# Second wo block in quarters back to back, both transposes and logits behind it, norms interleaved differently

## The chip, the cores and the metric

The kernel runs on one core of one Trainium2 chip. The metric is the device time of a launch in microseconds. Three runs of the kernel before took 1452.72 to 1453.64 us, 1453.02 us in the median.

## The reference

One layer of a hybrid encoder block on 256 tokens of width 1024, in f32. A first part (input projection, chunked attention, a state-space branch, cross-attention) ends in `merged`. The second part is a mixture of experts. The stretch between them is what this case is about:

```python
x = x + merged @ w_out[l]
# moe_ffn(rms_norm(x, norm_ffn[l]), ...):
logits = (xt @ w_router + b_router).astype(jnp.float32)
top_val, top_idx = lax.top_k(logits, TOP_K)          # 4 of 32
wts = jax.nn.softmax(top_val, axis=-1)
# tokens are sorted into blocks by expert; for each block:
g = jnp.minimum(xblk @ w_gate[e] + b_gate[e], SWIGLU_LIMIT)
u = jnp.clip(xblk @ w_up[e] + b_up[e], -SWIGLU_LIMIT, SWIGLU_LIMIT)
yb = ((u + 1.0) * g * jax.nn.sigmoid(SWIGLU_ALPHA * g)) @ w_down[e] + b_down[e]
```

## The kernel before

The tokens lie in two tiles of 128 (t = 0, 1). The first part is a list of weight blocks of 512 columns, each in four quarters of 256 input rows. A quarter ("unit") is loaded, rounded by ScalarE (`split`), its rest is taken by VectorE or GpSimd (`rest`), and TensorE runs three passes with the two parts (`three_passes`, L1589 to L1593). A list written out by `schedule()` (L93 to L208) orders everything: each engine walks it and does its own share of each step. `at(w, ...)` puts a step behind unit w. The last two blocks are `("wo", 0)` and `("wo", 1)`, the two column halves of w_out.

Block wo1 is special. The steps of the list run its four quarters for token tile 0 only; the four quarters of tile 1 (`second_tile(q)`) are written behind the list. Between them lie the transposes of x (step `outT` for columns 0 to 511 of both tiles, `turn_out(t)` for the rest of tile t) and the router's products (step `logits` for the first four chunks of both tiles, `last_logits(t)` for the last four). TensorE's order from wo1 on (L1868 to L1902) is: q0, q1, q2, `outT`, q3, `logits`, second 0, `turn_out(0)`, second 1, `last_logits(0)`, second 2, second 3, `open_sum(0, 0)`, `turn_out(1)`, count places of tile 0, `open_sum(1, 0)`, `last_logits(1)`, a small product, first gather, `open_sum(0, 1)`, two small products, second gather, `open_sum(1, 1)`, expert 0. (`open_sum` puts x into the bank that collects the result; `gather` collects the rows of expert 0 by a product with zeros and ones.)

VectorE (L1464 to L1483) does `add_out(t)` (x plus the product, for wo1's columns), `take_xT(t)` (copies transposes out of PSUM), `norm_begin(t)` (mean square), `choose(t)` (inverse root, scaled logits, top 8, row of zeros and ones), `find_first(t)` (hits of expert 0). ScalarE (L875 to L885) squares and sums a row's second half, takes the root, and scales the normed rows `h2`, tile by tile.

The expert weights come by SyncE's queue. An expert needs six loads of 2 MB in this order: gate, up, down, two halves of each. There are ten slots, and load k of expert e takes slot (6e+k) mod 10. In what follows (e,k) is load k of expert e, counted from 0. The queue (L569 to L600) waits before each load until its slot is free: load (1,0) for two quarters of wo1's tile 1 (`unit_used` at UNITS-2), (1,1) and (1,2) for all of it, (1,3) for the last logits, for `h2` and for the fourth `open_sum`, and from (1,4) on for the expert before to have used the slot. (2,2), for instance, takes slot 4, which the first down half of expert 0 holds.

Of the kernel before, what the change touches and what calls it, by code (L numbers as in the profile page):

```python
# [5 lines left out]
P = 128  # L6
# [5 lines left out]
ALU = mybir.AluOpType  # L12
# [80 lines left out]
def schedule():  # L93
# [104 lines left out]
    at(first("wo", 1) + 2, "outT")  # L198
    at(first("wo", 1) + 3, "logits")
# [45 lines left out]
def hybrid_block_kernel(nc, x, mem, g_mix, w_in, w_dt, a_gains, rel_rev, conv_w, conv_b, dt_bias, a_log, d_skip,  # L245
                        g_ssm, g_mem, w_mem_kv, x_gains, w_br_a, w_br_b, w_br_c, w_out, norm_ffn, w_router,
                        b_router, w_gate, b_gate, w_up, b_up, w_down, b_down, bias_dram, out):
    with ExitStack() as ctx:
# [420 lines left out]
        def _(act):  # L669
# [28 lines left out]
            for step in SCHED:  # L698
# [28 lines left out]
                elif kind == "take" and step[1] == "wo":  # L727
                    i = step[2]
                    cols = slice(i * NB, (i + 1) * NB)
                    for h in range(2):  # L730
                        act.wait_ge(gemm_taken, GEMM_AT[("wo", i, h)] + 1)
                        act.wait_ge(sem("br_merged"), 12)
                        act.activation(tmp[:, h], x_sb[:, h, cols], ACT.Square, accum_out=ss_part[:, 2 * i + h:2 * i + h + 1])\
                            .then_inc(sem("out_squares"), 1)
                elif kind == "take" and step[1:] != ("bc", 1):
# [139 lines left out]
            for t in range(TT):  # L875
                act.wait_ge(gemm_taken, GEMM_AT[("wo", 1, t)] + 1)
                act.wait_ge(sem("out_squares"), TT + t)
                act.activation(tmp[:, t], x_sb[:, t, NB:2 * NB], ACT.Square, accum_out=ss_part[:, TT + t:TT + t + 1])\
                    .then_inc(sem("out_squares"), 1)
                root(1)  # L880
                act.wait_ge(sem("second_norm"), t + 1)
                for h in range(2):
                    cols = slice(h * NB, (h + 1) * NB)
                    act.activation(h2[:, t, cols].rearrange("q (c p) -> q c p", c=4), interleaved(x_sb[:, t, cols]),
                                   ACT.Copy, scale=rs_2[:, t:t + 1]).then_inc(sem("h2_ready"), 1)  # L885
# [29 lines left out]
        def _(dve):  # L915
# [39 lines left out]
            def rstd_here(dst, src, width):  # L955
# [12 lines left out]
                return last  # L968

# [17 lines left out]
            for step in SCHED:  # L987
# [366 lines left out]
                elif kind == "take" and step[1] == "wo":  # L1354
# [4 lines left out]
                    for h in range(2):  # L1359
                        n = GEMM_AT[("wo", i, h)]  # L1360
                        dve.tensor_tensor(x_sb[:, h, cols], x_sb[:, h, cols], ps[:, GEMM_BANKS[n % 4], :], ALU.add)\
                            .then_inc(gemm_taken, 1)
                    dve.wait_ge(gain2_landed, 32)
                    dve.tensor_tensor(wr_sb[:], wr_sb[:], gain2_sb[:].unsqueeze(2).to_broadcast([P, KC, EXPERTS]),
                                      ALU.mult).then_inc(sem("router_scaled"), 1)
                elif kind == "outT":
                    for c2 in range(2):
# [29 lines left out]
            across = [P, TOP_K, EXPERTS]  # L1397

            def add_out(t):

                n = GEMM_AT[("wo", 1, t)]
                if t == 0:
                    dve.wait_ge(sem("wo_first_tile"), 1)
                else:
                    dve.wait_ge(unit_used, UNITS)
                dve.tensor_tensor(x_sb[:, t, NB:2 * NB], x_sb[:, t, NB:2 * NB], ps[:, GEMM_BANKS[n % 4], :], ALU.add)\
                    .then_inc(gemm_taken, 1)

            def take_xT(t):

                b = group()
                dve.tensor_copy(xT[:, 4:8, t * P:(t + 1) * P], ps[:, b, :].rearrange("p (c t) -> p c t", c=4))\
                    .then_inc(misc_taken, 1)

            def norm_begin(t):

                dve.wait_ge(sem("out_squares"), TT + t + 1)
                link(dve.tensor_tensor(ss_2[:, t:t + 1], ss_part[:, t:t + 1], ss_part[:, TT + t:TT + t + 1], ALU.add))
                variance(rs_2[:, t:t + 1], ss_2[:, t:t + 1], D)

            def choose(t):

                inverse_root(rs_2[:, t:t + 1]).then_inc(sem("second_norm"), 1)
                dve.wait_ge(sem("second_norm"), t + 1)
# [39 lines left out]
            add_out(0)  # L1464
            take_xT(0)
            norm_begin(0)
            choose(0)
            add_out(1)
            take_xT(1)
            norm_begin(1)  # L1470
            find_first(0)
# [89 lines left out]
        def _(pe):  # L1561
# [39 lines left out]

            pe.wait_ge(sem("masks"), 3)
            n = 0
            for step in SCHED:
# [8 lines left out]
                elif kind == "gemm":  # L1613
# [39 lines left out]
                    if closes:  # L1653
                        n += 2
                elif kind == "headT":
# [157 lines left out]
                elif kind == "outT":  # L1813
                    pe.wait_ge(gemm_taken, GEMM_AT[("wo", 0, 1)] + 1)
                    for c2 in range(2):
                        by_columns(lambda t: x_sb[:, t], c2)
                elif kind == "logits":
# [11 lines left out]

            def second_tile(q):  # L1830

                w = first("wo", 1) + q
                hi, lo = quarter(w)[1:]
                b = GEMM_BANKS[GEMM_AT[("wo", 1, 1)] % 4]
                for c in range(2):
                    k = 2 * q + c
                    last = three_passes(ps[:, b, :], (mergedT[0][:, k, P:T], mergedT[1][:, k, P:T]),
                                        (hi[:, c], lo[:, c]), k == 0, k == KC - 1)
                last.then_inc(unit_used, 1)

            def turn_out(t):

                b = group()
                pe.wait_ge(gemm_taken, GEMM_AT[("wo", 1, t)] + 1)
                for c in range(4):
                    last = turn(ps[:, b, c * P:(c + 1) * P], x_sb[:, t, (4 + c) * P:(5 + c) * P])
                last.then_inc(misc_ready, 1)
# [20 lines left out]
            second_tile(0)  # L1868
            turn_out(0)
            second_tile(1)  # L1870
            last_logits(0)
            second_tile(2)
            second_tile(3)
            pe.wait_ge(gemm_taken, GEMM_AT[("wo", 1, 0)] + 1)
            open_sum(0, 0)
            turn_out(1)
# [4 lines left out]
            pe.wait_ge(gemm_taken, GEMM_END)  # L1881
            open_sum(1, 0)
            last_logits(1)
# [176 lines left out]
```

## Time and profile before

| what | value |
|---|---|
| median of three runs | 1453.02 us |
| the profiled execution, its own time | 1452.76 us |
| its span | 1450.6 us |
| TensorE busy | 1426.2 us (98%) |
| VectorE / ScalarE / GpSimd busy | 587.3 / 405.6 / 63.2 us |
| moved by DMA | 491.27 MB, mean 339 GB/s |
| expert 0 starts on TensorE | 536.84 us |

The span is the time between the first and the last recorded instruction; the device time of the same execution is 2.2 us longer. Times inside the trace are from the start of the span. TensorE is recorded as busy while a matmul is in its pipeline, so a high share doesn't say that it runs at its peak. The DMA row counts how much of the core's 16 DMA engines was busy.

### The profile page before, as it was taken

The numbers are of one execution on the slowest core, as the hardware profiler recorded it, in microseconds if no ns is written. First come the engines' busy times: TensorE is split into PE (matmuls) and PEld (weight loads), VectorE is DVE, ScalarE is ACT, GpSimd is POOL, SyncE is SP. The second block draws the span as 40 slices with busy tenths as digits, with TensorE's granted clock in tenths as the row PEclk, the third lists the DMA queues.
The fourth block names the chain that finished last, engine by engine and source line by source line (L and its number), as shares of the span: only waits on it lengthen the run. The fifth ranks groups of instructions, "written<-read, shape, count | busy, mean of one in ns | idle before, by whom it ended". The sixth has DMA issues, their size and how long they took to land.

```text
span 1450.6 us, 18622 instructions
## 1 busy us (share of the span) xinstructions
PE 1426.2 (98%) x7575; PEld 820.9 (57%) x7575; DVE 587.3 (40%) x1149; ACT 405.6 (28%) x601; POOL 63.2 (4%) x50
## 2 busy tenths in 40 slices
PE   6999999999999999999999999999999999999998
PEld 6898888877788864444444444444444444433433
DVE  5779788677788651211111121121212111111111
ACT  5766666556644531101010110101011011101100
POOL 5120000111100000000000000000000000000000
PEclk9999999999999999999999999999999999999999
DMA  7455444654573979999999999999999999999997
GB/s 253 141 187 176 158 144 151 209 164 160 174 269 130 381 282 422 430 427 427 427 430 428 427 427 430 429 427 428 429 429 428 428 429 428 427 428 429 429 426 295
DMA packets 74000, 491.27 MB, mean 339 GB/s; under 512 B 5264, under 2 KB 8976, under 8 KB 49376
## 3 DMA queue, kind: packets, MB, share of 16 engines
q1 hardware_dynamic: 71280, 487.57, 83.1%
q10 hardware_dynamic: 2160, 2.62, 0.6%
q8 instruction: 32, 0.52, 0.1%
q0 software_dynamic: 512, 0.43, 0.1%
q14 instruction: 16, 0.13, 0.0%
HBM read 488.93 MB, written 1.07 MB: 338 GB/s over the span
## 4 chain that ended last, share of the span: by engine, by line
PE 82%; DMA 9%; DVE 5%; ACT 2%; issue 1%; DVEq 0%; ACTq 0%; SPq 0%
PE ps L1930 26%; PE ps L1968 13%; PE ps L1591 8%; PE ps L1593 8%; PE ps L1592 8%; PE ps L1858 7%; DMA regions<-in_w_gate 6%; PE ps L1578 4%; PE ps L1910 4%; DMA regions<-in_w_up 3%; DVE regions L1166 2%; DVE splits L1020 1%; PE ps L1805 1%; PE ps L1938 1%; ACT splits L707 1%
## 5 line engine op out<-in xcount | busy, mean ns | idle before, releaser
L1930 PE MATMUL ps<-regions,sig 128*64 128x512 f32 x2048 | 463.3, 594 | 4.1 <-DMA regions<-in_w_gate 3.8
L1930 PEld LDWEIGHTS ps<-regions,sig 128*64 128x64 f32 x2048 | 141.7, 137 | 276.7 <-issue 260.1
L1968 PE MATMUL ps<-regions,tmp 128*64 128x512 f32 x1024 | 225.1, 592 | 0.0
L1591 PE MATMUL ps<-splits,regions_r 128*128 128x512 f32 x512 | 205.9, 402 | 0.1
L1593 PE MATMUL ps<-splits,regions_r 128*128 128x512 f32 x512 | 200.1, 391 | 0.0
L1592 PE MATMUL ps<-splits,regions_r 128*128 128x512 f32 x512 | 199.8, 390 | 0.0
L707 ACT ACTIVATE splits<-halves 128x1024 fp32r<-128x1024 f32 x152 | 159.1, 1056 | 95.9 <-PE ps L1593 81.0
L1020 DVE TENSOR_TENSOR splits<-halves,splits 128x1024 fp32r<-128x1024 f32 x132 | 161.1, 1224 | 43.5 <-ACT splits L707 42.2
L893 ACT ACTIVATE work<-work 128x512 f32<-128x512 f32 x32 | 20.1, 629 | 474.9 <-DVE work L1518 474.9
L1968 PEld LDWEIGHTS ps<-regions,tmp 128*64 128x64 f32 x1024 | 71.7, 137 | 132.0 <-issue 129.6
L1858 PEld LDWEIGHTS ps<-craw,regions 128*128 128x128 f32 x1024 | 119.2, 192 | 25.6 <-issue 25.2
L1858 PE MATMUL ps<-craw,regions 128*128 128x64 f32 x1024 | 124.7, 275 | 0.4 <-DVE craw L1445 0.4
L1523 DVE TENSOR_SCALAR work<-ps 128x512 f32<-128x512 f32 x32 | 22.1, 692 | 239.7 <-PE ps L1930 239.7
L1591 PEld LDWEIGHTS ps<-splits,regions_r 128*128 128x128 f32 x512 | 96.2, 188 | 22.5 <-issue 3.9
L1593 PEld LDWEIGHTS ps<-splits,regions_r 128*128 128x128 f32 x512 | 96.1, 188 | 20.9
L1532 DVE COPY sig<-ps 128x512 f32<-128x512 f32 x32 | 22.1, 692 | 211.1 <-PE ps L1968 211.1
L1592 PEld LDWEIGHTS ps<-splits,regions_r 128*128 128x128 f32 x512 | 96.3, 188 | 18.4
L898 ACT ACTIVATE tmp<-ps 128x512 f32<-128x512 f32 x32 | 19.1, 597 | 303.1 <-PE ps L1578 303.1
L1518 DVE TENSOR_SCALAR work<-ps 128x512 f32<-128x512 f32 x32 | 22.1, 692 | 176.8 <-PE ps L1930 176.8
L1910 PE MATMUL ps<-sig,craw 64*128 64x512 f32 x264 | 65.6, 615 | 0.8 <-DVE sig L1532 0.8
L662 POOL TENSOR_TENSOR splits<-halves,splits 128x1024 fp32r<-128x1024 f32 x20 | 48.5, 2425 | 330.7 <-ACT splits L707 330.7
L1591 PE MATMUL ps<-regions_r,splits 128*128 128x256 f32 x192 | 55.5, 289 | 0.0
(299 smaller groups left out, 1188.4 us busy)
## 6 DMA issues: line engine op xcount, KB each, us to landing
regions<-in_w_gate SPq DMA_DIRECT2D x64, 2048.0 KB, 29.1
regions<-in_w_up SPq DMA_DIRECT2D x64, 2048.0 KB, 27.4
regions<-in_w_down SPq DMA_DIRECT2D x64, 2048.0 KB, 30.2
halves<-in_w_in SPq DMA_DIRECT2D x48, 1024.0 KB, 5.1
halves<-in_w_br_b SPq DMA_DIRECT2D x8, 1024.0 KB, 5.0
halves<-in_w_mem_kv SPq DMA_DIRECT2D x8, 1024.0 KB, 5.0
halves<-in_w_br_a SPq DMA_DIRECT2D x4, 1024.0 KB, 5.2
halves<-in_w_br_c SPq DMA_DIRECT2D x4, 1024.0 KB, 7.5
```

What stands on the lines that cost most here:

```text
L662: pool.tensor_tensor(lo, raw, hi.bitcast(F32), ALU.subtract).then_inc(lo_ready_pool, 1)
L707: act.activation(hi, raw, ACT.Copy).then_inc(hi_ready, 1)
L1020: dve.tensor_tensor(lo, raw, hi.bitcast(F32), ALU.subtract).then_inc(lo_ready, 1)
L1166: ins = dve.scalar_tensor_tensor(out=acc, in0=src, scalar=cw_sb[:, c, tap:tap + 1], in1=acc, op0=ALU.mult, op1=ALU.add)
L1578: return pe.transpose(dst, src, ident[:])
L1591: pe.matmul(out, lhs[0], rhs[0], start=start, stop=False, skip_group_check=True)
L1592: pe.matmul(out, lhs[1], rhs[0], start=False, stop=False, skip_group_check=True)
L1593: return pe.matmul(out, lhs[0], rhs[1], start=False, stop=stop, skip_group_check=True)
L1858: last = pe.matmul(ps[:, X_BANK, c * BLK:(c + 1) * BLK], h2[:, t, c * P:(c + 1) * P], hot[:, t], start=(t == 0 and c == 0), stop=(t == TT ...
L1910: last = pe.matmul(ps[:, ACC[2 * t + h], :], hot_wT[rows, t], yb[rows], start=False, stop=False, skip_group_check=True)
L1930: last = pe.matmul(ps[64 * h:64 * h + 64, bank, :], xgT[:, 4 * k + c], eslots[slot][:, c, h * NB:(h + 1) * NB], start=(k == 0 and c == 0), ...
L1968: last = pe.matmul(ps[64 * h:64 * h + 64, D_BANK, :], actT[:, c, 64 * k:64 * k + 64], eslots[slot][:, c, h * NB:(h + 1) * NB], start=False ...
```

## The change

In the list, the quarters of wo1's tile 1 become steps of kind `second`: quarters 0 and 1 stand behind quarter 1 of tile 0, quarters 2 and 3 behind its quarter 3. `outT` and `logits` move behind the last unit. `outT` takes in both `turn_out`s on TensorE, and on VectorE the adds and the first norm: `add_out(0)`, `norm_begin(0)`, `add_out(1)`, `norm_end(0)`, then the copies. The multiplication of the router's weights by the gain is a step of its own in block bc0. ScalarE takes a root of one number in step `picks`, which loads the table of roots there, and later does both squares and roots before both row scalings.

The helper functions move to where the steps can call them, unchanged but for `choose`, whose first two lines become `norm_end`. The core of the diff:

```diff
@@ schedule()
     at(first("wo", 1), "picks")
-    at(first("wo", 1) + 2, "outT")
-    at(first("wo", 1) + 3, "logits")
+    for q in range(2):
+        at(first("wo", 1) + 1, "second", q)
+        at(first("wo", 1) + 3, "second", q + 2)
+    at(UNITS, "outT")
+    at(UNITS, "logits")
+    at(first("bc", 0) + 1, "router_scale")
@@ ScalarE
+                elif kind == "picks":
+                    act.activation(root_out[:, 31:32], ident[:, 0:1], ACT.Sqrt).then_inc(sem("root_warm"), 1)
...
                 act.activation(tmp[:, t], x_sb[:, t, NB:2 * NB], ACT.Square, accum_out=ss_part[:, TT + t:TT + t + 1])\
                     .then_inc(sem("out_squares"), 1)
                 root(1)
+            for t in range(TT):
                 act.wait_ge(sem("second_norm"), t + 1)
@@ VectorE
+            def norm_end(t):
+                inverse_root(rs_2[:, t:t + 1]).then_inc(sem("second_norm"), 1)
+                dve.wait_ge(sem("second_norm"), t + 1)
...
+                elif kind == "router_scale":
                     dve.wait_ge(gain2_landed, 32)
                     dve.tensor_tensor(wr_sb[:], wr_sb[:], gain2_sb[:].unsqueeze(2).to_broadcast([P, KC, EXPERTS]),
                                       ALU.mult).then_inc(sem("router_scaled"), 1)
                 elif kind == "outT":
+                    add_out(0)
+                    norm_begin(0)
+                    add_out(1)
+                    norm_end(0)
                     for c2 in range(2):
...
             def choose(t):
-                inverse_root(rs_2[:, t:t + 1]).then_inc(sem("second_norm"), 1)
-                dve.wait_ge(sem("second_norm"), t + 1)
...
-            add_out(0)
             take_xT(0)
-            norm_begin(0)
-            choose(0)
-            add_out(1)
             take_xT(1)
             norm_begin(1)
+            norm_end(1)
+            choose(0)
             find_first(0)
             choose(1)
@@ TensorE
+                elif kind == "second":
+                    second_tile(step[1])
...
                         by_columns(lambda t: x_sb[:, t], c2)
+                    turn_out(0)
+                    turn_out(1)
                 elif kind == "logits":
...
-            second_tile(0)
-            turn_out(0)
-            second_tile(1)
             last_logits(0)
-            second_tile(2)
-            second_tile(3)
-            pe.wait_ge(gemm_taken, GEMM_AT[("wo", 1, 0)] + 1)
+            pe.wait_ge(gemm_taken, GEMM_END)
             open_sum(0, 0)
-            turn_out(1)
+            pe.wait_ge(sem("logits_taken"), 1)
+            last_logits(1)
 
             b = group()
             pe.wait_ge(sem("chosen_ready"), 1)
             pe.matmul(ps[:, b, 0:EXPERTS], upto_r[:], chosen_r[:, 0], start=True, stop=True).then_inc(misc_ready, 1)
-            pe.wait_ge(gemm_taken, GEMM_END)
             open_sum(1, 0)
-            last_logits(1)
```

## Rows read from the trace of the kernel before

**Rows 1.** Chain of waits, near its end: start us, duration us, engine or transfer

```profile
1374.12 45.20 DMA regions<-in_w_gate
```

**Rows 2.** Windows: length, busy us (instructions) of each engine, granted clock, DMA share, GB/s

```profile
517.00:518.00 1.00, 1.00 (x7) 0.82 (x6) 1.00 (x2) 0.00 (x0) 0.00 (x0) 1.00 0.00 0
530.00:535.00 5.00, 4.63 (x36) 4.05 (x36) 3.45 (x20) 3.82 (x4) 0.00 (x0) 1.00 1.02 436
600.00:628.10 28.10, 28.10 (x152) 11.94 (x150) 5.48 (x11) 2.89 (x4) 0.00 (x0) 1.00 1.01 427
1359.00:1387.10 28.10, 27.29 (x144) 11.40 (x142) 5.31 (x11) 2.89 (x4) 0.00 (x0) 1.00 1.01 429
```

**Rows 3.** Timeline of SyncE's queue: issue of loads (1,0), (1,3), (2,1), (2,2)

```profile
523.55 0.33 SPq L509 DMA_DIRECT2D regions<-in_w_gate  x1
...
536.97 0.33 SPq L509 DMA_DIRECT2D regions<-in_w_up  x1
...
554.67 0.33 SPq L509 DMA_DIRECT2D regions<-in_w_gate  x1
...
562.75 0.33 SPq L509 DMA_DIRECT2D regions<-in_w_up  x1
```

**Rows 4.** DMA issues, the same four loads in order: size, us from issue to landing

```profile
regions<-in_w_gate SPq DMA_DIRECT2D x1, 2048.0 KB, 7.5
...
regions<-in_w_up SPq DMA_DIRECT2D x1, 2048.0 KB, 9.8
...
regions<-in_w_gate SPq DMA_DIRECT2D x1, 2048.0 KB, 11.7
...
regions<-in_w_up SPq DMA_DIRECT2D x1, 2048.0 KB, 8.8
```

**Rows 5.** Timeline of TensorE, 512 to 537 us: start us, us, line, operation

```profile
512.01 0.39 PE L1591 MATMUL ps<-splits,regions_r 128*128 128x512 f32 x1
...
516.09 1.03 PE L1578 MATMUL ps<-ident,regions 128*128 128x128 f32 x8
...
530.46 1.98 PE L1858 MATMUL ps<-craw,regions 128*128 128x64 f32 x16
...
536.84 3.65 PE L1930 MATMUL ps<-regions,sig 128*64 128x512 f32 x16
```

**Rows 6.** Chain of waits, 515 to 537 us: TensorE's steps

```profile
516.25 0.87 PE ps L1578 x8
...
518.53 1.71 PE ps L1598 x16
...
523.52 0.81 PE ps L1598 x8
...
528.67 0.95 PE ps L1865 x2
```

**Rows 7.** Timeline of VectorE, 515 to 527 us

```profile
516.73 1.29 DVE L1369 COPY regions<-ps 128x512 f32<-128x512 f32 x2
...
523.38 0.16 DVE L944 RECIPROCAL stat<-stat 128x1 f32<-128x1 f32 x1 [0.27 <-ACT stat L675]
...
524.15 0.16 DVE L948 TENSOR_TENSOR stat<-stat 128x1 f32<-128x1 f32 x1
...
524.45 0.25 DVE L1426 SCALAR_TENSOR_TENSOR rt<-ps,stat,head_rows 128x32 f32<-128x32 f32 x1
...
525.79 0.40 DVE L1436 TENSOR_REDUCE chosen_r<-work 128x32 fp32r<-128x128 f32 x1
```

**Rows 8.** Timeline of ScalarE, 519 to 527 us

```profile
519.28 0.63 ACT L878 ACTIVATE tmp<-regions 128x512 f32<-128x512 f32 x1 [2.79 <-DVE regions L1406]
...
520.02 1.28 ACT L675 ACT_TABLE_LOAD   x1
523.14 0.20 ACT L675 ACTIVATE stat<-stat 128x1 f32<-128x1 f32 x1 [1.83 <-DVE stat L936]
524.35 2.31 ACT L884 ACTIVATE regions<-regions,stat 128x512 f32<-128x512 f32 x2 [1.00 <-DVE stat L948]
```

More of the change, by code:

```diff
@@ L968, in rstd_here, with add_out, take_xT, norm_begin @@
                 return last
+            across = [P, TOP_K, EXPERTS]
+            def add_out(t):
+                n = GEMM_AT[("wo", 1, t)]
+                if t == 0:
+                    dve.wait_ge(sem("wo_first_tile"), 1)
+                else:
+                    dve.wait_ge(unit_used, UNITS)
+                dve.tensor_tensor(x_sb[:, t, NB:2 * NB], x_sb[:, t, NB:2 * NB], ps[:, GEMM_BANKS[n % 4], :], ALU.add)\
+                    .then_inc(gemm_taken, 1)
+            def take_xT(t):
+                b = group()
+                dve.tensor_copy(xT[:, 4:8, t * P:(t + 1) * P], ps[:, b, :].rearrange("p (c t) -> p c t", c=4))\
+                    .then_inc(misc_taken, 1)
+            def norm_begin(t):
+                dve.wait_ge(sem("out_squares"), TT + t + 1)
+                link(dve.tensor_tensor(ss_2[:, t:t + 1], ss_part[:, t:t + 1], ss_part[:, TT + t:TT + t + 1], ALU.add))
+                variance(rs_2[:, t:t + 1], ss_2[:, t:t + 1], D)
+            def norm_end(t):
+                inverse_root(rs_2[:, t:t + 1]).then_inc(sem("second_norm"), 1)
+                dve.wait_ge(sem("second_norm"), t + 1)
             dve.wait_ge(sem("masks"), 3)
@@ L1394, in _ @@
                             .then_inc(sem("br_merged"), 1)
[L1397 to L1419, printed above, removed]
             def choose(t):
-                inverse_root(rs_2[:, t:t + 1]).then_inc(sem("second_norm"), 1)
-                dve.wait_ge(sem("second_norm"), t + 1)
                 dve.wait_ge(sem("logits_ready"), t + 1)
@@ L1600, in router, with second_tile, turn_out @@
                 return last
+            def second_tile(q):
+                w = first("wo", 1) + q
+                hi, lo = quarter(w)[1:]
+                b = GEMM_BANKS[GEMM_AT[("wo", 1, 1)] % 4]
+                for c in range(2):
+                    k = 2 * q + c
+                    last = three_passes(ps[:, b, :], (mergedT[0][:, k, P:T], mergedT[1][:, k, P:T]),
+                                        (hi[:, c], lo[:, c]), k == 0, k == KC - 1)
+                last.then_inc(unit_used, 1)
+            def turn_out(t):
+                b = group()
+                pe.wait_ge(gemm_taken, GEMM_AT[("wo", 1, t)] + 1)
+                for c in range(4):
+                    last = turn(ps[:, b, c * P:(c + 1) * P], x_sb[:, t, (4 + c) * P:(5 + c) * P])
+                last.then_inc(misc_ready, 1)
             pe.wait_ge(sem("masks"), 3)
@@ L1827, in _ @@
                         by_columns(lambda t: merged[:, t], c2)
[L1830 to L1847, printed above, removed]
             def last_logits(t):
```

## The prediction

> **What bounds the kernel now.** I read the chain of waits first, at its end. It consists there of array work and of expert loads that were issued about 45 us before they landed, such as the last gate half that is waited for [rows 1]. The windows over one expert say the same from the other side [rows 2]. At 600 us the array is busy for all of 28.1 us and the loads run at 427 GB/s. At 1359 us the array is busy for 27.29 of 28.1 us and the loads still run at 429 GB/s. An expert is six loads of 2.097 MB, so the loads need 6 x 2.097/0.429 = 29.3 us for it (4.89 us each), while the array wants 28.1 us. The array falls back onto the stream of loads late, and from then on the loads end the kernel. What counts is therefore when the stream became dense and stayed dense. It stands still around 517 us [rows 2], as no slot is free.
>
> Call the loads (expert, number). The queue's times [rows 3] and the times to landing [rows 4] give: (1,0) issued 523.55, landed 531.05; (1,3) issued 536.97, landed 546.77; (2,1) issued 554.67, landed 566.37; (2,2) issued 562.75, landed 571.55. The last step is 5.18 us, 0.29 us more than a dense load takes. So the stream is dense from 523.55 on, but only just: (2,2) comes 0.29 us too late. (2,2) waits for slot 4, freed by the first down half of expert 0, so its issue moves with the start of expert 0 (536.84 [rows 5]). Two gates stand one behind the other at nearly the same price: the issue of (1,0), and the start of expert 0. The end moves earlier only if both do, and later if the second does.
>
> The other loads behind it leave room. (3,2) is issued one array period after (2,2), 590.86, while the dense stream reaches it 29.3 us later, so its margin is 1.2 us larger, and each further period adds as much.
>
> **The change part by part.**
>
> *Order of the second wo block.* A quarter of one token tile is six matmuls. 18 of them lie between 512.01 and the start of the transposes at 516.09 [rows 5], 0.2267 us each, so 1.36 us a quarter. After the change the array does q0, q1, second 0, second 1, q2, q3, second 2, second 3 without anything between. Second 1 starts its last matmul at 512.01+23x0.2267 = 517.22 and ends it 0.39 later, 517.6. So (1,0) goes out at about 517.65, 5.9 us earlier. The first tile is complete at 512.01+35x0.2267+0.39 = 520.33, the second at 512.01+47x0.2267+0.39 = 523.06. Then (1,1) and (1,2) go out, 4 us earlier than now.
>
> *The first norm with the second sum inside.* VectorE adds tile 0 from 520.36. ScalarE squares it, 0.74 us up to its next instruction [rows 8], so done near 521.83. The variance needs two small operations of 0.19, to 522.2. The root is 0.2 us. VectorE's next instruction is the add of tile 1, at 523.09, and the normalisation stands behind it. The add leaves VectorE after 0.60 us. The five operations of the inverse root take 523.38 to 524.31 [rows 7], 0.93 us. So norm 0 is done at 523.69+0.93 = 524.62.
>
> *Transposes and copies.* Array: eight transposes 0.87, four 0.44 (half of it) [rows 6], from 522.89 to 524.1. The last four need the first copy out of PSUM. VectorE's four copies step by 0.60 us (two take 1.29 with 0.69 the last [rows 7]). They start at 524.66; the first ends at 525.35, the second at 525.96. Array: four transposes 525.4 to 525.9, then the first half of the logits, 1.71 us [rows 6], from 526.0 to 527.7, then four chunks for tile 0, 0.81 us [rows 6]. They end, with the last one's drain, at 528.7, and VectorE sees them at 528.8. Meanwhile VectorE leaves the last copy at 527.06, has variance 1 at 527.4, and the root comes back at 527.65. Norm 1 ends at 528.6. Both arms meet at 528.8 within 0.2 us.
>
> *First choice and first gather.* From the scaled logits to the chosen row is 524.45 to 526.19 [rows 7], 1.74 us, so 530.54. Behind the logits of tile 0 (which leave room for the next work at 528.5) the array opens a sum, 0.95 us [rows 6], and computes the logits of tile 1, again 0.81 us; it is busy to about 530.3 and waits 0.3 us. Then it counts places (0.1), opens the next sum (0.95), does one more small product (0.1) and starts the first gather at 530.6+1.15 = 531.75. Now it starts at 530.46 [rows 5]. Everything from here to expert 0 is the same sequence: gather, open, places, VectorE's find, gather, open. The second choice (from 531.4 to 533.1) stays ahead of its use at 533.9. So expert 0 starts about 1.3 us later, at 538.1.
>
> *A second way to the same number.* Between 512.01 and 536.84 the array is idle now for only 0.4 us; 0.37 of it is the rest of the 5 us from 530 to 535 [rows 2]. The change leaves its work as it is. It adds idle time: 1.3 us before the last transposes, 0.15 before the logits, 0.3 before the places, 1.75 in all, so 1.75-0.4 = +1.3 us. The same count bounds the gain: with no idle at all, expert 0 could start at most 0.4 us earlier.
>
> *The root's table.* Its load of 1.28 us lies at 520.02 [rows 8], and the root begins only at 523.14, 1.8 us after the load ended. Hidden now, hidden then: 0. Below nothing is excluded, as no one waits for it. If it had no cover it would cost 1.28.
>
> *Squares in front of row scalings.* The scalings of tile 0 (2.31 us for two [rows 8]) now wait behind the second root: 527.7 to 530.0, tile 1 to 532.4. Their readers are the gathers at 531.75 and about 535.3. Cost 0, with 1.7 us of cover for tile 0. Exp's table load comes behind them; its result is needed after the gathered rows. Nothing is gained on the array's path either, since the second root is asked for by VectorE's fourth copy.
>
> *Router gain moved to bc0.* Its one VectorE operation costs less than one copy of 0.69 us [rows 7]. It is worth 0 saved in wo1, where it stood ahead of adds that wait for the array, and 0 in bc0, where the array works from quarters prepared ahead. If that cover failed it would cost up to 0.69.
>
> **The sum at the end.** (1,3) waits for the last opened sum and goes out at 538.3. Its predecessors landed by about 536.5, so the stream now stands still before it. Alone a load takes between 7.5 and 9.8 us (the extremes of [rows 4] with a short queue). (1,3) lands between 545.8 and 548.1; five dense loads later is 570.3 to 572.6. (2,2) goes out at 564.05 and can't land before 571.55 (by 7.5) or 572.85 (by 8.8). Against 571.55 now the end shifts by 0 to +1.3. The late (2,2) of today was itself not covered by the stream, so 8.8 is nearest to a true lone time. I take +1.2. The extra time in front of the first weights is lost, and the 5.9 us by which (1,0) is earlier buy nothing.
>
> [...]
>
> The profiled execution took 1452.76 us around a span of 1450.6, the three timed runs 1453.02 in the median, 0.26 above it. 1452.76+1.2 = 1453.96 in its own terms, so 1454.2 us as a median.
>
> **The rivals.**
>
> *No shift (1453.1).* As above, with the lone load at 7.5 us. For it: (1,0) showed 7.5. Against: (2,2) was late already at 8.8.
>
> *Faster: the stream's start decides (1447.1).* If the end followed (1,0) alone it would come 5.9 us earlier. For it: the stream is dense from 523.55 on. Against: (2,2) can't be issued before expert 0 frees its slot, and the idle count allows 0.4 us there.
>
> *Slower: the chain of handovers is longer (1456.5).* From the end of the last wo matmul to the first gather VectorE, ScalarE and the array take turns about twelve times, each at 0.03 to 0.1 us in my sum. With 0.2 us a turn and one missed near-tie, expert 0 is 3.5 us late. It decides as soon as expert 0 starts 2.9 us late. Against: every handover has a row now, and the same operations.
>
> *Slower: the array's clock (1460.5).* Every window shows granted 1.00 (2.4 GHz), also 530 to 535 with 0.37 us idle. If the gap of 1.3 us brought it to 1.2 GHz, the 6.3 us of array work from the first gather to expert 0 would take up to 12.6, +7.6 with the 1.3. Against: the whole stretch of small products shows 1.00 now.
> The Trainium skill (TensorE: Matmul & The Clock Gate, Why this matters for your kernels) warns of idle gaps between bursts of matmuls as what lowers the clock; no run here shows such a gap.
>
> *The change does less than it says.* The table loaded ahead is such a part; it is in the sum at 0.
>
> **How the numbers follow.** Forecast 0.70, no shift 0.14, faster 0.04, long chain 0.06, clock 0.06. A measurement of this kernel can tell about 0.2%, 2.9 us, from no change. Faster 0.04, within 0.2% 0.84, slower 0.12. The range 1452.4 to 1456.3 holds both of the first two with the runs' spread of 0.9, and ends at the edge of the long chain.
>
> **What would show it.** (1,0) issued near 517.6; the stream standing still before (1,3); the first gather near 531.8, with 1 to 1.5 us of idle array before the last four transposes; expert 0 at 538.1; (2,2) landing 0 to 1.3 us later. Expert 0 before 536.4 would refute the idle count. An end several us earlier with a late expert 0 would refute that (2,2) binds. Windows below 1.00 between 524 and 540 would be the clock.

## The result and the profile after

| | runs | median us | lowest to highest |
|---|---|---|---|
| before | 17 | 1452.83 | 1451.80 to 1453.64 |
| changed | 17 | 1460.52 | 1454.15 to 1463.82 |
| changed, taken again | 5 | 1460.38 | 1454.06 to 1463.44 |

The recorded ratio is 1.0045 (95% interval 1.0038 to 1.0053); it is the ratio of the means, and that of the medians is 1.0053. So the kernel is slower, and the median lies outside the forecast's range of 1452.4 to 1456.3. The times of the changed kernel fall into two groups. In 6 of its 22 runs TensorE's granted clock has a mean of 1.00, and the times are 1454.06 to 1454.44 us. In the other 16 the mean is 0.992 to 0.994, and the times are 1459.78 to 1463.82 us. The kernel before showed no such second group here. I call the 16 the runs with the fall. The two groups have to be read apart: one bears on the forecast's sum, the other on a rival.

The clock's row of the page of the changed kernel (40 slices of 36.5 us, granted clock in tenths) shows where to look:

```profile
PEclk9999999999999979999999999999999999999999
```

The windows of the same run give the place. Columns: stretch, length, busy time and count of TensorE's products, of its weight loads, of VectorE, ScalarE, GpSimd; granted clock, DMA share, GB/s. They answer to [rows 2].

```profile
520.00:525.00 5.00, 4.01 (x24) 3.26 (x23) 3.09 (x11) 1.65 (x5) 0.00 (x0) 1.00 0.96 374
525.00:530.00 5.00, 4.94 (x30) 3.84 (x31) 4.00 (x18) 2.92 (x4) 0.00 (x0) 0.85 1.01 429
530.00:535.00 5.00, 5.00 (x19) 3.87 (x17) 2.33 (x11) 3.17 (x4) 0.00 (x0) 0.50 0.83 357
535.00:540.00 5.00, 4.84 (x18) 3.70 (x17) 0.59 (x4) 0.00 (x0) 0.00 (x0) 0.50 0.00 0
545.00:550.00 5.00, 5.00 (x15) 1.52 (x16) 3.39 (x19) 0.00 (x0) 0.00 (x0) 0.61 0.77 259
```

The clock goes from 2.4 to 1.2 GHz (1.00 to 0.50) inside the second window, stays there for some 20 us and comes back in the last. The loads stand still from 535 on, because (1,3) waits for the fourth opened sum. Windows of the run taken again, in which the clock stayed:

```profile
525.00:530.00 5.00, 4.03 (x30) 3.54 (x31) 4.08 (x14) 2.10 (x5) 0.00 (x0) 1.00 0.96 387
530.00:535.00 5.00, 4.77 (x32) 3.78 (x31) 3.11 (x16) 4.12 (x5) 0.00 (x0) 1.00 0.98 419
```

TensorE's timeline, first in the run with the fall, then in the run without. It answers to [rows 5].

```profile
522.54 1.47 PE L1593 MATMUL ps<-ident,regions 128*128 128x128 f32 x12
525.06 0.66 PE L1593 MATMUL ps<-ident,regions 128*128 128x128 f32 x4 [1.05 <-DVE regions L1412]
525.65 2.87 PE L1613 MATMUL ps<-wr_sb,regions 128*128 128x32 f32 x24
...
533.80 3.65 PE L1877 MATMUL ps<-craw,regions 128*128 128x64 f32 x16
545.30 5.45 PE L1943 MATMUL ps<-regions,sig 128*64 128x512 f32 x16
```

```profile
523.45 1.47 PE L1593 MATMUL ps<-ident,regions 128*128 128x128 f32 x12
525.97 0.66 PE L1593 MATMUL ps<-ident,regions 128*128 128x128 f32 x4 [1.04 <-DVE regions L1412]
526.56 2.87 PE L1613 MATMUL ps<-wr_sb,regions 128*128 128x32 f32 x24
532.49 1.98 PE L1877 MATMUL ps<-craw,regions 128*128 128x64 f32 x16
538.86 3.65 PE L1943 MATMUL ps<-regions,sig 128*64 128x512 f32 x16
```

The first gather takes 3.65 us instead of 1.98. From its start to expert 0 it is 11.5 us instead of 6.4. The whole trace of the first run lies 0.35 us earlier than that of the kernel before, and that of the second 0.56 later: the transposes start at 522.54 and 523.45 where I put them at 522.89, and SyncE's load of 500.06 goes out at 499.71 and 500.62. I call this shift the base of a trace. With it taken off, expert 0 starts at 545.65 and 538.30, against 536.84 before. So it is 8.8 us late with the fall and 1.46 us late without. The spans are 1459.2 and 1451.9 us against 1450.6, or 1459.6 and 1451.3 with the base taken off.

The issues of (1,0), (1,3), (2,1) and (2,2) on SyncE's queue in the run without the fall, and then the microseconds in which (1,3), (2,1) and (2,2) landed, answer to [rows 3, 4]:

```profile
518.20 0.33 SPq L513 DMA_DIRECT2D regions<-in_w_gate  x1
...
538.99 0.33 SPq L513 DMA_DIRECT2D regions<-in_w_up  x1
...
556.70 0.33 SPq L513 DMA_DIRECT2D regions<-in_w_gate  x1
...
564.77 0.33 SPq L513 DMA_DIRECT2D regions<-in_w_up  x1
```

```profile
regions<-in_w_up SPq DMA_DIRECT2D x1, 2048.0 KB, 8.6
...
regions<-in_w_gate SPq DMA_DIRECT2D x1, 2048.0 KB, 10.8
...
regions<-in_w_up SPq DMA_DIRECT2D x1, 2048.0 KB, 7.6
```

(1,3) lands at 547.59, 11.5 us behind (1,2): there the stream stood still. (2,1) lands at 567.50 and (2,2) at 572.37, 4.87 us later. So (2,2) was issued while (2,1) was still on its way, and it took one dense step.

### The profile page after: what moved, and what is told of

Read it like the earlier page. It is cut to its first block, busy times and chain, and to the rows that moved or that the text cites. A ratio compares the mean times of both kernels' runs of the same rounds, so it can differ in the third digit from the quotient of the medians.

```text
span 1459.2 us, 18624 instructions
## 1 busy us (share of the span) xinstructions
PE 1434.5 (98%) x7575; PEld 826.5 (57%) x7575; DVE 590.1 (40%) x1149; ACT 405.8 (28%) x602; POOL 63.5 (4%) x50
## 4 chain that ended last, share of the span: by engine, by line
PE 82%; DMA 9%; DVE 5%; ACT 2%; issue 1%; ACTq 0%; SPq 0%
PE ps L1943 27%; PE ps L1981 13%; PE ps L1606 8%; PE ps L1608 7%; PE ps L1607 7%; PE ps L1877 7%; DMA regions<-in_w_gate 6%; PE ps L1923 4%; PE ps L1593 4%; DMA regions<-in_w_up 3%; DVE regions L1203 2%; DVE splits L1057 1%; PE ps L1841 1%; PE ps L1951 1%; ACT splits L711 1%
## 5 line engine op out<-in xcount | busy, mean ns | idle before, releaser
L1877 PEld LDWEIGHTS ps<-craw,regions 128*128 128x128 f32 x1024 | 122.5, 196 | 25.9 <-issue 25.7
L1877 PE MATMUL ps<-craw,regions 128*128 128x64 f32 x1024 | 128.1, 279 | 0.2 <-DVE craw L1462 0.2
```

What stands on the lines that cost most here:

```text
L1877: last = pe.matmul(ps[:, X_BANK, c * BLK:(c + 1) * BLK], h2[:, t, c * P:(c + 1) * P], hot[:, t], start=(t == 0 and c == 0), stop=(t == TT ...
```

## The experiments

After the first comparison I held theory I: in the forecast's words, the gap of 1.05 us before the last transposes lowers the clock. Its rival, theory L, was that the kind of work counts, the router's products of 32 columns above all. A second question was which gate holds the end when the clock stays. Each experiment was timed beside the kernel before on the same chip. Only one run of each kernel has a trace (of the changed kernel two). All counts of runs with the fall are by the mean clock and the time of each run, so a short fall in a run with a mean of 0.998 or 0.999 is not excluded by them; some runs of the kernel before have these means too.

**One wide product in the gap.** The changed kernel, with one unused product of 512 columns there.

```diff
+                    pe.matmul(ps[:, EXP_BANK, :], ident[:], x_sb[:, 0, 0:NB], start=True, stop=True)
```

> The changed kernel with one more product of x by the identity (128x512, f32, result unused) in the array's idle time before the last four transposes (1.05 us idle there in its trace, granted clock 1.00 before, 0.50 from 528.3 us on). Theory I (the idle time is what takes the clock down): the gap closes, every window shows 1.00, all runs at 1454.2 us. Theory L (the stretch of transposes and 32-column products takes it down, idle or not): this product is full-width work, so 1454.2 is possible under it too. Rival: the clock falls for neither reason, and runs stay split between 1454.2 and 1460 to 1464.

Ten runs: 5 with the fall (1459.84 to 1463.12), 5 without (1453.79 to 1454.45); ratio 1.0031 (1.0017 to 1.0046).

**Small transposes in the gap.**

```diff
+                    for c in range(9):
+                        turn(ps[:, EXP_BANK, 0:P], x_sb[:, 0, 0:P])
```

> The same place filled for the same 1 us by nine more 128x128 transposes (result unused). Theory I: the gap is closed, clock 1.00 throughout, 1454.2 us in all runs. Theory L: light work doesn't help, the granted clock falls to 0.50 near 528 us in most runs as in the changed kernel, median near 1460.5.

Twelve runs: 6 with the fall (1459.75 to 1463.80), 6 without (1453.32 to 1454.15); ratio 1.0028 (1.0012 to 1.0044). With the gap filled, by either kind of work, the fall still comes in half of the runs. So the gap isn't needed for it. Whether it adds to the chance (16 of 22 with it, 11 of 22 without) these counts don't decide; the next kernel, also without the gap, makes it 14 of 33 against 16 of 22, which speaks for some share of the gap.

**The gap taken away by order.** VectorE copies the first transposes before it ends norm 0; `norm_end(0)` moves behind the two copies, and nothing else changes.

> The changed kernel with VectorE's end of the first norm behind the first two copies, nothing else. The last four transposes no longer wait for it: the idle 1.05 us before them goes, and no work is put in. Theory I: clock 1.00, expert 0 some 0.9 us earlier than in an undisturbed run of the changed kernel (near 537.0), so 1453.3 us. Theory L: the stretch of light work is as long as before, the clock falls in most runs, median near 1459.5.

Eleven runs: 3 with the fall (1457.91 to 1462.93), 8 without (1452.63 to 1454.08); ratio 1.0014 (1.0001 to 1.0027). Expert 0 gained about 0.4 us: VectorE's copies moved, and norm 0, which the first choice needs, moved back.

**The gap alone.** The kernel before, with a write of 128x1024 numbers on VectorE ahead of `add_out(1)`, so that the array waits.

```diff
+                    dve.memset(work[:, 0:2], 0.0)
```

> The kernel before, with a VectorE memset of 128x1024 ahead of its second sum, so that the array idles about 1 us before its last four transposes, right behind two quarters of full-width products and an opened sum. Theory I: the clock falls to 0.50 in most runs, 1460 us or more. Theory L: the clock stays at 1.00, expert 0 is about 1 us late and the end with it: 1453.8 us (between 1453.0 and 1454.0).

No fall in 11 runs, 1452.91 to 1455.33, median 1454.19; ratio 1.0006 (0.9997 to 1.0015). Its timeline shows the gap, as long as in the changed kernel:

```profile
528.76 0.63 PE L1579 MATMUL ps<-ident,regions 128*128 128x128 f32 x4 [1.03 <-DVE regions L1407]
```

Theory I falls with this as the whole cause: an idle array of 1.03 us ahead of the same transposes did not lower the clock in any run. Here it stands behind products of 512 columns and no long row of logits follows, so that the gap helps such a row is not excluded.

**The changed kernel's gain without its long stretch.** The kernel before, with quarters 0 and 1 of tile 1 early (so (1,0) goes out at 516.98, or 517.65 with the base taken off), and quarters 2 and 3 still between the transposes and the router's products; `add_out(1)` ahead of `choose(0)`, and `open_sum(1, 0)` ahead of the places.

```diff
+    for q in range(2):
+        at(first("wo", 1) + 1, "second", q)
...
-            second_tile(0)
-            turn_out(0)
-            second_tile(1)
-            last_logits(0)
```

> The kernel before with the quarters of tile 1 at the changed kernel's places only for 0 and 1 (behind q1); quarters 2 and 3 stay between the transposes and the logits, so no stretch of light work is longer than before. VectorE adds tile 1 before the first choice. Theory L (long light stretch takes the clock down): 1.00 in every run. Theory of two gates: load (1,0) goes out near 517.5 as in the changed kernel, expert 0 starts at 536.5 to 536.9, and since (2,2) still comes with expert 0, the end gains only 0 to 0.4 us: 1453.0 against 1453.3 of before. Rival (the start of the stream alone decides): 1447.4. Rival (the early quarters or loads take the clock down): runs near 1460.

A miss: all 5 runs had the fall, 1457.17 to 1460.32, median 1458.19; ratio 1.0036 (1.0023 to 1.0050). The windows show the place:

```profile
528.00:530.00 2.00, 1.33 (x7) 0.65 (x6) 1.42 (x4) 2.00 (x4) 0.00 (x0) 1.00 0.98 418
530.00:532.00 2.00, 1.78 (x14) 1.68 (x14) 1.62 (x10) 0.54 (x4) 0.00 (x0) 0.86 0.97 418
532.00:534.00 2.00, 2.00 (x12) 2.00 (x11) 1.39 (x8) 2.00 (x2) 0.00 (x0) 0.50 0.94 401
```

The opened sum that used to stand between logits and places was gone from there. From 528.6 to 530.94 the array did only products of 32 columns and waits, and behind them stood the gather. That this is the cause is a reading after the fact; the kernel with the small products filled up, below, tests it.

**Expert 0 frees its slots sooner.** The kernel before, with expert 0's scatter into the opened sums left out. That scatter is 1.9 us of array work that adds a product with zeros, so the result stays the same.

```diff
-                scatter(i)
+                if not opening:
+                    scatter(i)
```

> The kernel before without expert 0's first scatter, 1.92 us of array work that adds a product with zeros (the result is unchanged); TensorE's first round of experts is written out for it. Expert 0's down half, and with it (2,2), comes 1.9 us earlier, (1,0) does not. Two gates: the dense stream from (1,0) takes over at once, gain 0.3 us, 1453.0. Rival (expert 0 alone decides): gain 1.9 us, 1451.4.

No fall in 11 runs, median 1453.09 against 1453.11; ratio 1.0001 (0.9992 to 1.0010). The issue and the landing of (2,2):

```profile
559.75 0.33 SPq L509 DMA_DIRECT2D regions<-in_w_up  x1
...
regions<-in_w_up SPq DMA_DIRECT2D x1, 2048.0 KB, 10.3
```

The base of this trace is 1.05 us early (the load of 500.06 goes out at 499.01). With that taken off, (2,2) is issued at 560.80, 1.95 us earlier than before, and lands at 571.10, 0.45 us earlier [rows 3, 4] and 4.87 us behind (2,1), a dense step. So the issue of (2,2) alone isn't the gate; the start of the stream stands close behind it.

**Both gates opened.** The last two edits together; the scatter of zeros in expert 0 is left out here too.

> Both: the quarters as in e5_hybrid and expert 0 without its scatter. Two gates: now both move, (2,2) by 1.9 to 2.3 us, (1,0) by 5.9, so the end gains about 2.1 us: 1451.2. Rival (gains are what e5 and e6 give, added): at most 0.7 us, 1452.6. Rival (array pace, not loads, sets the end): gain 1.9 in e6 and e7 alike.

All 7 runs had the fall, 1456.68 to 1458.14; ratio 1.0031 (1.0020 to 1.0042). It says nothing on the gates.

**A stretch of small work with no idle time.** The kernel before, with 12 unused transposes and 24 unused products of 32 columns (48 instructions, as each f32 product is two) ahead of the first opened sum.

```diff
+            for c in range(12):
+                turn(ps[:, ACC[2], 0:P], x_sb[:, 0, 0:P])
+            for c in range(24):
+                pe.matmul(ps[:, ACC[2], 0:EXPERTS], xT[:, c % 8, 0:P], wr_sb[:, 0], start=True, stop=True)
```

> The kernel before with 12 transposes and 24 products of 32 columns (results unused) ahead of its first opened sum, about 4.0 us more of light work in one piece and no idle time added. Theory L: the clock falls to 0.50 in a good part of the runs, these near 1463; the others are late by 4.0 us, 1457.3. Theory I (idle time is needed): clock 1.00 in all, 1457.3.

The times are 1460.63 to 1461.60; ratio 1.0054 (1.0040 to 1.0068). I count all 5 as runs with the fall: the traced one shows it from the second window below to about 538 us, the others have a mean clock of 0.997 to 0.999 and the same times. The added work is longer than the 4.0 us that I had expected, some 6.6 us at the full clock; the fall's part of the time is not measured by itself. The timeline of the added products and three windows:

```profile
527.36 6.61 PE L1878 MATMUL ps<-wr_sb,regions 128*128 128x32 f32 x48
```

```profile
528.00:530.00 2.00, 2.00 (x20) 2.00 (x19) 0.00 (x0) 0.00 (x0) 0.00 (x0) 1.00 1.06 451
530.00:532.00 2.00, 2.00 (x18) 2.00 (x17) 0.00 (x0) 0.00 (x0) 0.00 (x0) 0.85 0.94 401
532.00:534.00 2.00, 2.00 (x11) 2.00 (x11) 0.00 (x0) 0.00 (x0) 0.00 (x0) 0.50 0.96 410
```

The array is recorded busy for 2.00 of 2.00 us in each window, and the clock falls all the same. So the fall needs no idle array. The Trainium skill (TensorE: Matmul & The Clock Gate, HAM oscillation — how this bites in real kernels) puts the slow clock of thin matmuls down to the waits for DMA between them, during which the array idles. This kernel had no such wait in these windows and fell, so the page's cause is not the only one.

**Opened sums back among the small products.** The changed kernel, with `open_sum(1, 0)` in the gap between the last transposes, `open_sum(0, 0)` between the two tiles' logits and `open_sum(0, 1)` ahead of the first gather. The middle edit:

```diff
-                    for t in range(TT):
-                        router(t, 0)
+                    router(0, 0)
+                    pe.wait_ge(gemm_taken, GEMM_AT[("wo", 1, 0)] + 1)
+                    open_sum(0, 0)
+                    router(1, 0)
```

> The changed kernel with its opened sums (full-width products it does anyway) moved into the stretch of light work: (1,0) between the last two groups of transposes, where the array idled 1.05 us, (0,0) between the logits of the two tiles, (0,1) ahead of the first gather. Nothing added. Longest piece without a full-width product falls from 5.8 us to about 3 us. Theory L: clock 1.00 in nearly all runs, expert 0 about 1 us earlier than in an undisturbed run of the changed kernel, near 537.0, end at 1453.2 against about 1453.2 of before. Rival (a low share of array work over the whole 12 us up to expert 0, however it is spread, or another cause): still split, half the runs at 1458 or more.

Nine of 11 runs with the fall (1456.84 to 1459.70), 2 counted as without (1454.84, 1455.01, with a mean clock of 0.999); ratio 1.0029 (1.0020 to 1.0038). Moving the sums thinned out the place behind. Logits, a wait, logits, a wait and the places now follow one another for 4 us, and only one opened sum and a small product stand between them and the gather:

```profile
528.03 1.87 PE L1613 MATMUL ps<-wr_sb,regions 128*128 128x32 f32 x16
530.37 1.05 PE L1613 MATMUL ps<-wr_sb,regions 128*128 128x32 f32 x8 [0.47 <-issue]
531.89 0.25 PE L1897 MATMUL ps<-chosen_r,upto_r 128*128 128x32 f32 x1 [0.47 <-DVE chosen_r L1453]
531.99 1.10 PE L1630 MATMUL ps<-regions,ident 128*128 128x512 f32 x2
532.53 0.58 PE L1900 MATMUL ps<-chosen_r,ones_r 128*128 128x32 f32 x1
532.96 3.40 PE L1885 MATMUL ps<-craw,regions 128*128 128x64 f32 x16
```

The same with expert 0's scatter left out:

> e10_spread and expert 0 without its scatter of zeros (result unchanged). Two gates: (1,0) is 5.9 us early and (2,2) 1.8 us, so with the clock at 1.00 the end gains 1.5 to 2 us on the kernel before: 1451.5. If the clock falls in a run, 1457 or more. Rival (loads don't bind at (2,2)): same time as e10_spread.

All 6 runs with the fall, 1457.86 to 1458.95; ratio 1.0034 (1.0021 to 1.0046).

**Both gates, and the small products filled up.** The kernel with both gates opened, and in addition `open_sum(0, 1)` ahead of the first gather and two unused products of 256 columns in the waits.

```diff
+            pe.matmul(ps[:, ACC[3], 0:T], ident[:], x_sb[:, 0, 0:T], start=True, stop=True)
...
+            open_sum(0, 1)
```

> e7_both (quarters 0 and 1 of tile 1 early, no scatter in expert 0), which fell to 0.50 in every run, with full-width work brought between its light work: the opened sum (0,1) ahead of the first gather, and two unused products of 256 columns, one in each of its waits. Theory L: clock 1.00 in most runs, 1451.5. Rival (the order of quarters takes the clock down, not what follows them): 1457 as e7_both.

The traced run shows 1.00 from 520 to 556 us, and the other ten have a mean clock of 0.999 or 1.00, where the same kernel without the fillings had the fall in 7 of 7 (on another chip). For the clock this is the cleanest pair. For the time it is a miss: 1452.37 to 1455.81, median 1453.51 against 1453.12; ratio 1.0002 (0.9993 to 1.0011). The traced run is the slowest of the eleven. Its mean is 0.998, since the clock fell once near the end, where the array waits for loads (the window from 1420 to 1425 shows 0.66, with the array busy for 3.83 of 5.00 us). The issues of (1,3) and (2,2) and their landings say why nothing was gained:

```profile
538.12 0.33 SPq L511 DMA_DIRECT2D regions<-in_w_up  x1
...
561.96 0.33 SPq L511 DMA_DIRECT2D regions<-in_w_up  x1
```

```profile
regions<-in_w_up SPq DMA_DIRECT2D x1, 2048.0 KB, 7.7
...
regions<-in_w_up SPq DMA_DIRECT2D x1, 2048.0 KB, 9.4
```

(2,2) lands at 571.36, 25.5 us behind (1,3) at 545.82: four steps of 4.85 to 4.97 us and one of 5.85. But (1,3) lands 7.0 us behind (1,2), which shows that the stream had stood still before it. (1,3), which waits for the last opened sum, had become the stream's start, and it is a third gate.

**The two small parts alone.** The kernel before, with the root's table loaded in the step `picks` and the router's gain applied in bc0.

```diff
+    at(first("bc", 0) + 1, "router_scale")
...
+                elif kind == "picks":
+                    act.activation(root_out[:, 31:32], ident[:, 0:1], ACT.Sqrt).then_inc(sem("root_warm"), 1)
```

> The kernel before with two of the small parts of the change alone: the root's table loaded in step picks, and the router's weights scaled in block bc0. My sum gives both 0: 1453.1 and clock 1.00. Rival (the table load or the scaling was on the path): 1.3 us faster or 0.4 us slower.

No fall in 11 runs, median 1453.20 against 1453.12; ratio 0.9999 (0.9990 to 1.0008). Both together are worth nothing that these runs can show, as forecast.

**Wide products or transposes in three places.** The changed kernel, with one unused product of 512 columns in the gap, one between the two tiles' logits and one behind them; and its twin with nine transposes in each of the same places, which take about the same time.

```diff
+                    pe.matmul(ps[:, ACC[2], :], ident[:], x_sb[:, 0, 0:NB], start=True, stop=True)
```

> The changed kernel with three unused full-width products (128x512, 0.95 us each): in the idle time before the last transposes, between the logits of the two tiles and behind them. The second and third cost time, so expert 0 starts about 1.5 to 1.9 us later than in an undisturbed run of the changed kernel. Theory L (too little full-width work between the last quarter and expert 0 takes the clock down): clock 1.00 in most runs, these at 1455.7 to 1456.1, faster in the median than the changed kernel. Rival (timing, not width): falls in as many runs as e15_narrow.

> The same with nine 128x128 transposes (1 us) at each of the three places. Theory L: the clock falls in at least as many runs as in the changed kernel, median 1461 or more. Rival: as e14_wide, whatever that shows.

Neither fell, in 11 runs each (mean clock 0.999 or 1.00). Wide: 1454.77 to 1457.48, median 1455.74; ratio 1.0021 (1.0012 to 1.0030). Transposes: 1454.49 to 1456.44, median 1455.62; ratio 1.0017 (1.0008 to 1.0026). That the transposes held the clock as well I had not expected. Two lines of their timeline:

```profile
527.10 1.18 PE L1593 MATMUL ps<-ident,regions 128*128 128x128 f32 x9
528.12 0.98 PE L1613 MATMUL ps<-wr_sb,regions 128*128 128x32 f32 x8
```

An instruction of 128 columns and one of 32 columns both take about 0.11 us here, so the transposes pass four times as many columns in the same time.

**One kind of small work at a time.** The kernel before, with about 3.7 us of a single kind ahead of the first opened sum: 16 unused products of 32 columns (32 instructions), or 32 unused transposes.

```diff
+            for c in range(16):
+                pe.matmul(ps[:, ACC[2], 0:EXPERTS], xT[:, c % 8, 0:P], wr_sb[:, 0], start=True, stop=True)
```

> The kernel before with 16 unused products of 32 columns (32 matmul instructions, 3.5 us) ahead of its first opened sum. Theory T (long pieces in which the array streams few columns, products of 32 columns or waiting, take the clock down): the clock falls in at least part of the runs; disturbed ones above 1458, the others at 1453.1+3.5 = 1456.6. Theory W (anything that isn't a weight quarter or a full-width product): the same in e17_turns.

```diff
+            for c in range(32):
+                turn(ps[:, ACC[2], 0:P], x_sb[:, 0, 0:P])
```

> The kernel before with 32 unused 128x128 transposes (3.5 us) at the same place. Theory T: clock 1.00 in all runs, 1456.6. Theory W: falls as often as e16_thin.

The windows of the products of 32 columns, then those of the transposes:

```profile
530.00:532.00 2.00, 2.00 (x13) 1.80 (x13) 0.00 (x0) 0.00 (x0) 0.00 (x0) 0.74 1.00 426
532.00:534.00 2.00, 2.00 (x7) 1.06 (x5) 0.00 (x0) 0.00 (x0) 0.00 (x0) 0.50 1.01 434
```

```profile
530.00:532.00 2.00, 2.00 (x15) 1.56 (x14) 0.00 (x0) 0.00 (x0) 0.00 (x0) 1.00 0.95 401
532.00:534.00 2.00, 2.00 (x13) 1.27 (x11) 1.20 (x6) 0.20 (x1) 0.00 (x0) 1.00 1.01 434
```

The first fell in its profiled run (1458.15), while its other ten took 1454.48 to 1456.58, at a mean clock of 1.00; ratio 1.0015 (1.0006 to 1.0024). The second showed 1.00 throughout, 1455.10 to 1456.95; ratio 1.0018 (1.0009 to 1.0027). This is in the expected direction, but one run in 11 is weak evidence.

**All kernels together.** The column "piece" is the longest stretch from the first transposes to the first gather in which the array did only products of 32 columns or waited, read from each timeline (in the kernel before it is the first row of logits). "Sum" is an opened sum, a product of 512 columns.

| kernel | piece, us | runs with the fall |
|---|---|---|
| before, scatter left out, gap alone, the two small parts alone | 1.9 | 0 of 17, 0 of 11, 0 of 11, 0 of 11 |
| 32 transposes added | 1.9 | 0 of 11 |
| both gates, filled up | 1.9 | 0 of 11 |
| wide or transposes in three places | 1.3 | 0 of 11, 0 of 11 |
| changed; with the gap filled; with it moved | 2.9 | 16 of 22; 5 of 10, 6 of 12, 3 of 11 |
| 16 products of 32 columns added | 3.9 | 1 of 11 |
| gain without the stretch, both gates | 2.3, then the gather | 12 of 12 |
| sums moved, with and without scatter | 4.0, then one sum and the gather | 15 of 17 |
| 24 products of 32 columns and 12 transposes added | 6.6 | 5 of 5 |

The kernels with pieces of up to 1.9 us never fell; those with longer ones did, but not in the order of their length. What follows the piece seems to count as well. Where the gather with its products of 64 columns follows directly, the fall came in 12 of 12 runs; with one opened sum between them, in 15 of 17; with two opened sums and eight more instructions of 32 columns between them, as in the changed kernel, in 30 of 55. No pair of kernels tests this by itself, and the 1 of 11 with 16 added products shows that it is not the whole rule. The early quarters and loads of the change are not the cause: the kernels with added products of 32 columns fell without them, and the two with three filled places have them and never fell.

## Why the prediction was wrong

*The sum was right, as far as it went.* Without the fall each of its steps is in the trace. With the base taken off, (1,0) goes out at 517.64 (forecast 517.65), the gap is 1.04 us (1.3), the first gather starts at 531.93 (531.75), and expert 0 at 538.30 (538.1). The stream stands still before (1,3), (2,2) is late with expert 0, and the time is 1454.06 to 1454.44 us (1454.2). So the 5.9 us by which (1,0) was earlier bought nothing, by the cause given. But the last step came right partly by luck. I took 8.8 us for (2,2) as the time of a load that is alone. It never was alone: before, (2,1) was still on its way for 3.6 us of the 8.8, and now for 2.7 of the 7.6. A load that was alone is (1,0), at 7.5 us both times. In the changed kernel (2,2) took one dense step behind (2,1), so in this trace (1,3) was the gate, issued 1.5 us later than before with the base taken off. (2,2) landed at 571.81, 0.3 us late instead of 1.2. The rest of the loss came further on: (3,0) landed 5.77 us behind the load ahead of it, where a dense step is 4.9, and no term of the sum stands for that. The span grew by 0.7 us with the base taken off, the median of the six runs by 1.4. My reading of the kernel before had the same flaw: I called its stream dense from 523.55 on, but (1,3) landed 5.9 us behind (1,2) there, a full microsecond over a dense step. Single steps of 5.2 to 5.9 us stand at changing places in the traces, so the 0.29 us that I read as (2,2)'s lateness is within what one step varies. In two other traces (the gap filled with a wide product, and the gap alone) (2,2) itself landed 6.97 us behind (2,1); how much it adds in a given run stays open.

*The step that failed is the chance of the clock rival.* I gave it 0.06, with the sentence "the whole stretch of small products shows 1.00 now". That put the clock's cost at nothing in the sum. Its price as a rival (1460.5) met the median of 1460.52, though not by its own terms: in the traced run expert 0 is 8.8 us late instead of 7.6. Of that 5.1 us lie between the first gather and expert 0, where I had 6.3, and 2.2 lie in front of the gather, where I had nothing. As for the step itself, I read the windows of the kernel before as if they showed the new stretch. They don't. Before, the logits came in rows of 16, 8 and 8 instructions, with products of 512 columns between them. The change moves those products ahead, so that 24 instructions of 32 columns stand in a row, 2.87 us, behind a gap. No window of before held such a row, and its 1.00 couldn't speak for it. In 16 of 22 runs the clock fell there.

*The rival's cause was wrong too.* I hung it on the gap. The gap alone did nothing (0 of 11), and filling it left the fall (11 of 22), though it may add to the chance. A stretch of small products lowered the clock in 5 of 5, with the array busy throughout in the traced run. Wide products or transposes between the logits kept it (0 of 22).

*The rest.* "No shift" and "faster" did not come. The long chain did not come: the handovers cost what the rows said. The squares and scalings, the table and the gain in bc0 cost nothing.

*What stays open.* What the clock goes by is not settled. Every kernel that fell between 520 and 535 us has a piece of products of 32 columns or waits that is longer than the 1.9 us of the kernel before. But pieces of 2.9 us fell in some runs of one program and not in others, and the piece of 3.9 us added to the kernel before fell only once in 11. Why the same program takes either course was not found. The Trainium skill (TensorE: Matmul & The Clock Gate, What's actually happening) says that the monitor runs free of the kernel's start, so that a kernel meets it at another phase in each run; the two courses of one program agree with that, but no trace here shows the monitor. No kernel of this study beat the kernel before; those whose interval holds 1 have ratios of 0.9999, 1.0001, 1.0002 and 1.0006, and none of them holds the whole change.

## What to carry to other kernels

When a change gathers an array's narrow work into one row, the products it moves away may have held the clock up; a granted clock of 1.00 over the mixed stretch says nothing about the row that is left. Price that rival by the array work behind it (here 6.4 us became 11.5), take a chance well above "never seen", and run the kernel many times, since one run of the changed kernel would have told either story. And where two waits stand at nearly the same price in front of a dense stream, opening one can show the next: here there were three. Take the time of a lone load from one that had the queue to itself.

## What the runs showed of the hardware

- An f32 transpose of 128x128 and one instruction of an f32 product of 32 columns with 128x128 weights both step by about 0.11 us, so 32 columns are as dear as 128; such a product is two instructions. 32 transposes in a row (3.65 us), behind work at the full clock, kept it at 1.00. The Trainium skill (TensorE: Matmul & The Clock Gate, Part 4: PE-mode transpose) says that the full clock doesn't engage for transposes; the runs here decide.
- The clock fell with the array at 2.00 of 2.00 us busy (24 products of 32 columns added), and stayed through 1.03 us idle (the gap alone, 0 of 11).
- A fall lasted about 20 us in the changed kernel and cost 5.7 to 9.4 us of the end; in the kernel with 16 added products it was back by 535 us and cost about 3 (1458.15 against a median of 1454.98).
- An expert load with an empty queue took 7.5 us for 2.097 MB ((1,0), before and changed), against about 4.9 us a load in the dense stream.
